# Routing of a 32-expert layer rebuilt: the second norm applied as one factor per token, logits accumulated between the projection's tiles, token rows added onto a shift row in DRAM by DMA, and slot lists found by rounding

## The reference, cut to what matters

```
x  = x + gt1 * (concat([attn, conv]) @ w_out)          # the projection w0..w7
h2 = rmsnorm(x, g_norm2) * (1.0 + sc2) + sh2           # second norm, gain, shift

logits = h2 @ w_router + b_router                      # 512 x 32
top_logit, top_idx = lax.top_k(logits, 4)
gate = softmax(top_logit)
# each expert's tokens are padded up to whole blocks of 128 slots
counts = zeros(32).at[flat_e].add(1)
padded = (counts + 127) // 128 * 128
pad_end = cumsum(padded)
slot = pad_start[e_sorted] + arange(n_pair) - start[e_sorted]
slot_tok, slot_gate = ...                              # for each slot its token and gate
block_expert = searchsorted(pad_end, block_start, side='right')

for each block:  xb = h2[tok];  y = swiglu(xb @ w_gate_up[e] + b) @ w_down[e] + b;  out[tok] += y * gate
x = x + gt2 * out;  final rmsnorm
```

## Time and profile before

| | |
|---|---|
| median of 3 runs | 2510.17 us (2509.6 to 2510.8) |
| profiled execution | 2509.06 us, its span 2507.2 us |
| PE busy in the span | 2416.3 us (96%) |
| DVE, ACT, POOL busy | 2024.9 (81%), 1320.3 (53%), 678.6 us (27%) |
| granted TensorE clock, mean | 0.98 of full speed |

### The profile page before, as it was taken

How to read it: one execution, slowest core, us unless ns; L and a number is a source line. 1 busy time by engine, 2 the same in 40 slices (tenths; PEclk the granted TensorE clock), 3 DMA queues, 4 the chain that set the end, 5 groups by cost and what they waited for, 6 DMA issues and landing times.

```text
span 2507.2 us, 31686 instructions
## 1 busy us (share of the span) xinstructions
PE 2416.3 (96%) x10915; PEld 1944.6 (78%) x10915; DVE 2024.9 (81%) x1856; ACT 1320.3 (53%) x1206; POOL 678.6 (27%) x407
## 2 busy tenths in 40 slices
PE   8999999999999999999869999999999999999995
PEld 7777788786877877878657888888888888888884
DVE  7787577576885786885269999999999999999994
ACT  4442233334323234334247777777777777777772
POOL 5343341332433432341312122112111211221120
PEclk9999999999999999999879999999999999999997
DMA  6232245222422752230069999999999999999992
GB/s 237 84 125 77 67 152 185 67 76 72 147 68 76 267 208 72 69 100 1 13 240 363 378 365 371 368 377 364 367 367 377 366 366 373 371 368 366 377 358 88
DMA packets 104427, 572.48 MB, mean 228 GB/s; under 512 B 14192, under 2 KB 14336, under 8 KB 54288
## 3 DMA queue, kind: packets, MB, share of 16 engines
q1 hardware_dynamic: 86784, 515.15, 54.9%
q0 software_dynamic: 17280, 56.20, 7.9%
q10 hardware_dynamic: 288, 0.14, 0.0%
HBM read 559.37 MB, written 24.12 MB: 233 GB/s over the span
## 4 chain that ended last, share of the span: by engine, by line
PE 86%; DVE 7%; DVEq 2%; DMA 1%; ACT 1%; issue 1%; ACTq 0%; POOL 0%; SPq 0%; POOLq 0%
PE ps L1493 83%; PE ps L1171 2%; DVE scr L2354 1%; DVE scr L2194 1%; DMA scr<-in_ada 1%; DVEq L2356 1%; DVE y_split L2131 1%; PE ps L666 0%; DVE mix L2245 0%; DVE scr L2243 0%; DMA mix<-acc_rows 0%; PE ps L1423 0%; DVEq L2141 0%; DMA acc_rows<-rows,lst 0%; DVE w_split L1298 0%
## 5 line engine op out<-in xcount | busy, mean ns | idle before, releaser
L1298 DVE TENSOR_TENSOR w_split<-raw,w_split 128x2048 fp32r<-128x2048 f32 x386 | 877.3, 2287 | 54.3 <-ACT w_split L1250 43.3
L1493 PE MATMUL ps<-y_split,pieces_split 128*128 128x512 f32 x3600 | 844.6, 395 | 15.9 <-POOLq L2561 7.3
L1250 ACT ACTIVATE w_split<-raw 128x2048 fp32r<-128x2048 f32 x386 | 736.2, 1916 | 196.0 <-PE ps L1493 176.3
L1493 PEld LDWEIGHTS ps<-y_split,pieces_split 128*128 128x128 f32 x3600 | 679.9, 189 | 167.8 <-issue 26.1
L1493 PE MATMUL ps<-w_split,rows_T 128*128 128x512 f32 x3096 | 751.9, 393 | 1.9 <-DVE rows_T L1304 1.9
L1493 PEld LDWEIGHTS ps<-w_split,rows_T 128*128 128x128 f32 x3096 | 575.3, 188 | 119.4 <-DVE rows_T L1304 2.5
L2549 POOL TENSOR_TENSOR pieces_split<-pieces,pieces_split 128x1024 fp32r<-128x1024 f32 x151 | 372.3, 2476 | 646.4 <-ACT pieces_split L1827 518.5
L1827 ACT ACTIVATE pieces_split<-pieces 128x1024 fp32r<-128x1024 f32 x144 | 151.3, 1058 | 425.6 <-PE ps L1493 394.4
L1493 PE MATMUL ps<-w_split,hidden_T 128*128 128x512 f32 x1536 | 363.6, 392 | 2.0 <-DVE hidden_T L1304 1.7
L1493 PEld LDWEIGHTS ps<-w_split,hidden_T 128*128 128x128 f32 x1536 | 284.9, 188 | 74.6 <-DVE hidden_T L1304 15.0
L1362 POOL COPY rows_i<-slot_tokens 128x1 int32 (+1 forms) x34 | 60.9, 1790 | 412.9 <-PE ps L1171 379.4
(11 more groups left out here) (265 smaller groups left out, 2068.8 us busy)
## 6 DMA issues: line engine op xcount, KB each, us to landing
raw<-in_w_moe SPq DMA_DIRECT2D x386, 1024.0 KB, 7.6
pieces<-in_pieces SPq DMA_DIRECT2D x181, 512.0 KB, 3.6
scr<-in_ada POOLq DMA_DIRECT2D x48, 512.0 KB, 5.6
scr<-in_ple SPq DMA_DIRECT2D x2, 1536.0 KB, 6.9
acc_rows<-in_zeros POOLq DMA_DIRECT2D x5, 512.0 KB, 10.9
hT<-in_xT SPq DMA_DIRECT2D x8, 256.0 KB, 5.6
h_rows<-scr SPq DMA_DIRECT2D x4, 512.0 KB, 3.7
mix<-acc_rows SPq DMA_DIRECT2D x4, 512.0 KB, 5.1
```

Of the source, the lines that this page charges most:

```text
L1250: nc.scalar.activation(wsp[:, p % SPLIT, 0], raw[:, p % RAW, :], ACT.Copy).then_inc(high, 3 if p == 1 else 1)
L1298: nc.vector.tensor_tensor(wsp[:, p % SPLIT, 1], raw[:, p % RAW, :], wsp[:, p % SPLIT, 0].bitcast(F32), ALU.subtract).then_inc(low, 3 if p ...
L1493: return pe.matmul(out, lhsT, rhs, start=start, stop=stop)
```

## The change

The shift `sh2` and the norm's factor are taken out of the path. Per token t, with 1/std the norm's factor `r`, h2 = r * (hT * coef) + sh2. So:

- ACT squares each `hT` tile and scales it by `coef` (`gained`) while PE is in the next projection tile; DVE adds up squares 1 to 6 (`sq3`). PE puts the logits' matmuls of tile k between projection tiles (from w4 on). The sums of squares come by token: 128 tokens on partitions, one column. `r_col` is 128x4 instead of 128x512. Logits are r * (gained @ w) + (sh2 @ w + bias), the latter (`shifted_bias`) made during w5 and w6.
- Token rows: ACT copies the transposed `gained` with scale `r_col`. SP has earlier written `sh2` into a DRAM row (`shift_dram`, 1024 elements of 4 bytes) and copied it to all 513 rows of `h2_dram`; POOL now adds the rows onto it by four accumulating DMAs. Rows in DRAM are numbered from 1, so that 0 means an empty slot; the count of ones is dropped from `owner`.
- Slots: `pos` in 5 wider matmuls; block counts by rounding ((n + 63.5)/128, then adding and subtracting 1.5 * 2^23); the 50 block experts by one comparison against the partition's number, one sum, and one matmul of ones against a diagonal ("be").
- Lists: block and remainder of all 16 token/choice columns at once by rounding; `in_block` in one instruction of 800 columns, then two instructions per token tile (`owner` 400 columns, `place` 512), each in buffers of its own. List matmuls have 100 columns.
- The bias load (L1120) and its splitting move from after w7 to after w0 and w4; POOL's copies ahead of the first two gathers are gone.

```diff
 def tail_sp(sp):
     for t in range(A_RAW, len(TAIL)):
+        if t == A_RAW + 2:
+            sp.wait_ge(csum_ready, 1)
+            sp.dma_start(shift_dram[0, :].rearrange("(k p) -> p k", p=P), ada[:, SH2:SH2 + DK, 0], ...)
+        if t == A_RAW + 6:
+            sp.wait_ge(h2_init, 16)
+            sp.dma_start(h2_dram[:, :], shift_dram[0, :].partition_broadcast(ROWS))
...
-    for t in range(ST):
-        sp.wait_ge(h2n_ready, t + 1)
-        sp.dma_start(h2_dram[t * P:(t + 1) * P, :], h2n[:, t, :])

 # PE
 for m_ in range(DK):
     features(CV, f"w{m_}", ...)
+    if m_ == 4:
+        router[0] = direct_router()
+        mm(ps[:, 4, 0:ST * E_N], ident[:], zer..., True, False)
+        for k in range(4):
+            pe.wait_ge(norm2_ready, GAINED(k)); logits_of(k)
+    if m_ > 4:
+        pe.wait_ge(norm2_ready, GAINED(m_ - 1)); logits_of(m_ - 1)
+    if m_ == 6:
+        pe.wait_ge(route_ready, SHIFT)
+        mm(ps[:, 5, E_N:2 * E_N], ones[:], shift_sum, True, True)
+mm(ps[:, 5, 0:ST], ident[:], zer[:, 0:ST], True, False)
+token_sums(0, False)
+pe.wait_ge(norm2_ready, SQUARED(DK - 1)); token_sums(DK - 1, True)
+pe.wait_ge(route_ready, LAST_GAINED);     logits_of(DK - 1)

 # DVE, after the logits and the top four
-            nc.vector.tensor_tensor(reached, edges, slot..., ALU.is_le)
-            nc.vector.reduce_sum(first_past, reached, AX.X)
...
+nc.vector.tensor_scalar(base, slotf, -(P - 1) / 2, 1.0 / P, ALU.add, ALU.mult)
+nc.vector.tensor_scalar(base, base, WHOLE, -WHOLE, ALU.add, ALU.add)
+nc.vector.scalar_tensor_tensor(rem, base, -float(P), slotf, ALU.mult, ALU.add)
+nc.vector.tensor_tensor(in_block[:], iota, base..., ALU.is_equal)
+for t in range(ST):
+    nc.vector.tensor_tensor(owner[:, n0:n1], in_block..., value..., ALU.mult)
+    nc.vector.tensor_tensor(place[:, n0:n1, :], iota, rem..., ALU.is_equal)
+    dve.drain().then_inc(onehot_ready, 1)

 def experts_pool(pool):
+    pool.wait_ge(h2_init, 32)
+    for t in range(ST):
+        pool.wait_ge(h2n_ready, t + 1)
+        pool.dma_start(h2_dram[1 + t * P:1 + (t + 1) * P, :], h2n[:, t, :], accum_op=ALU.add)
...
-    fetch(0, 0)
-    fetch(1, 1)
+    rows_of(list_tok[:, 0:1], 0)
+    rows_of(list_tok[:, 1:2], 1)
```

More of the change, by code:

```diff
@@ L411, in build @@
         BA = Groups(nc, ctx, "ba", [4, 5, 6, 7], ba_order)
-        CV = Groups(nc, ctx, "cv", [0, 1, 2, 3, 4, 5], [f"w{i}" for i in range(DK)] + ["logits", "pos", "lists"])
-        CA = Groups(nc, ctx, "ca", [6, 7], ["norm2"] + [f"t{i}" for i in range(8)])
+        CV = Groups(nc, ctx, "cv", [0, 1, 2], [f"w{i}" for i in range(DK)] + ["pos", "be", "lists"])
+        CA = Groups(nc, ctx, "ca", [3, 6, 7], [f"t{i}" for i in range(8)])
         DV = Groups(nc, ctx, "dv", [0, 1, 2, 3, 4, 5], [f"t{i}" for i in range(8)])
@@ L975, in tail_dve @@
             dve.sem_inc(CA.free, len(CA.banks))
+            nc.vector.memset(chosen[:, 0, :], 0.0)
+            nc.vector.memset(chosen[:, ST + 1, :], 0.0)
+            nc.vector.memset(zer, 0.0)
+            dve.drain()
             for m in range(DK):
@@ L984, in tail_dve @@
+            dve.wait_ge(std2_ready, 9)
+            nc.vector.reciprocal(r_col, std_col)
+            dve.drain().then_inc(route_ready, 1)
+            dve.wait_ge(route_full, LOGITS)
+            for t in range(ST):
+                nc.vector.scalar_tensor_tensor(logits[:, t, :], ps[:, 4, t * E_N:(t + 1) * E_N], r_col[:, t:t + 1],
+                                               shifted_bias, ALU.mult, ALU.add)
             dve.drain()
-            x = full(CV, "logits")[:, 0:ST * E_N].rearrange("p (t e) -> p t e", t=ST)
@@ L988, in tail_dve @@
-            nc.vector.tensor_tensor(logits, x, brt[:].unsqueeze(1).to_broadcast([P, ST, E_N]), ALU.add)
-            dve.drain().then_inc(CV.free, 1)
             for t in range(ST):
@@ L1035, in tail_dve @@
[L1035 to L1041 removed]
+            nc.vector.tensor_scalar(be_diag, ident[:, 0:LISTS], be_col, None, ALU.mult).then_inc(route_ready, 1)
@@ L1047, in tail_dve @@
             nc.vector.tensor_tensor(h2k, hk, posn.unsqueeze(2).to_broadcast([P, ST, TOP, E_N]), ALU.mult)
-            dve.drain()
+            nc.vector.tensor_scalar(be_bc[:], full(CV, "be", LISTS), float(E_N - 1), None, ALU.min)
+            dve.drain().then_inc(CV.free, 1)
+            nc.vector.tensor_copy(be_r[:], be_bc[0:1, :]).then_inc(be_ready, 1)
+            dve.sem_inc(low, 2)
             nc.vector.reduce_sum(slotf, hot2, AX.X)
@@ L1069, in tail_dve @@
[L1069 to L1076 removed]
+                n0, n1 = t * TOP, (t + 1) * TOP
@@ L1077, in tail_dve @@
+                nc.vector.tensor_tensor(owner[:, n0:n1], in_block[:, n0:n1, :].unsqueeze(2).to_broadcast([P, TOP, 2, LISTS]),
+                                        value[:, n0:n1, :].unsqueeze(3).to_broadcast([P, TOP, 2, LISTS]), ALU.mult)
+                nc.vector.tensor_tensor(place[:, n0:n1, :], cst[:, 0:P].unsqueeze(1).to_broadcast([P, TOP, P]),
+                                        rem[:, n0:n1].unsqueeze(2).to_broadcast([P, TOP, P]), ALU.is_equal)
                 dve.drain().then_inc(onehot_ready, 1)
-            x = full(CV, "lists")[:, 0:3 * LISTS].rearrange("p (c b) -> p c b", c=3)
@@ L1116, in bias_sp @@
         def bias_sp(sp):
-            sp.wait_ge(CV.full, CV.done(0, "w7"))
+            sp.wait_ge(CV.full, CV.done(0, "w0"))
             for i in range(2):
@@ L1354, in experts_pool @@
         def experts_pool(pool):
+            pool.wait_ge(h2_init, 32)
+            for t in range(ST):
+                pool.wait_ge(h2n_ready, t + 1)
+                pool.dma_start(h2_dram[1 + t * P:1 + (t + 1) * P, :], h2n[:, t, :], accum_op=ALU.add).then_inc(h2_out, 16)
             n = block_pairs(pool)
```

288 lines of the change are left out of this document (164 added, 124 removed).

## The result

The changed kernel takes 2477.81 us (median of 4 runs, 2476.74 to 2478.55) against 2510.01 us for the kernel before on the same chip (4 runs, 2509.6 to 2510.8): a ratio of 0.9871, 95% interval 0.9854 to 0.9888. Its profiled execution took 2478.25 us with a span of 2476.4 us, 30.81 us less than the one of before. The prediction was 2477. Medians and ranges in this document are of fast executions; one of the four of warm_hold took 6280.96 us, has no trace, and is in neither.

What follows compares the result with a forecast made beforehand. One serial chain between projection and the PE-bound expert phase was taken to bound the gain: 40.5 us for 73.45, a gain of 33; 2509.06 - 33 = 2476.1, median 1.1 above, so 2477, range 2472 to 2486.

Steps and rivals of the forecast that it cites:

- half clock: Rival: small matmuls of stages 1, 2 and 4 leave gaps, clock falls; with slow gather 2482 to 2487, chance 0.14.
- stage 4: From the lists to POOL's gather issue: 7.9 us (7.0 to 9.5), 13.21 before.
- projection, added: Router matmuls put between projection tiles, on the path: 6.5 us added; bounds 6.0, or 12.9 at half-clock price.
- stage 1: From the last projection tile to the logits: 3.5 us (3.2 to 5 if the clock falls), 31.74 before.
- stage 2: From the logits to "pos": 5.9 us (5.4 to 7), 9.44 before.
- stage 3: From "pos" to the lists: 6.1 us (5.7 to 7), 9.32 before.
- stage 5: From POOL's gather to the first expert matmul: 10.6 us (8.7 to 14.9), 9.74 before; landing taken as 6.0.
- The first weight load: SP's expert weight loads start 1.9 us after the block experts are ready, at about 1243.5.
- Late rows: Rival: the accumulating row DMAs, not the lists, set the gather: 2484, or up to 2503; chance 0.13.
- the other side: Rival: accumulating DMAs take over 13.3 us each without overlap, a loss; 2517 at 15 each; chance 0.02.
- no change: Outcome given a chance of 0.01; a measurement tells 0.2%, 5 us, from it.
- After the first expert matmul: From the first expert matmul to the end: order as before, the same 1211 us.

Runs made afterwards that it cites:

- warm_hold: Changed kernel with weight loads 3 and 4 released only after the first rows' selection, plus six unread matmuls ahead of the lists: 2476.27 us (median of three), ratio 0.9866.
- router_behind: Changed kernel with the first seven tiles' router matmuls moved from the projection to behind w7: 2480.14 us, ratio 0.9881.
- control2: The changed kernel run once more, unedited, beside all_warm: 2477.97 us, ratio 0.9867.
- control: The changed kernel run once more, unedited, on one chip with rows_first, warm_hold and bias_in_routing: 2476.14 us, ratio 0.9868.
- warm_both: Changed kernel with unread 128x512 matmuls on PE, six ahead of the lists and eight ahead of the gathered rows: 2476.48 us, ratio 0.9865.
- all_warm: warm_hold's edits on the changed kernel, plus five unread matmuls ahead of the gathered rows and two after the first bias matmul: 2471.55 us, ratio 0.9842.
- plain_rows: Changed kernel with the four row DMAs writing plainly instead of adding onto the shift, so gathered rows lack it: 2474.42 us, ratio 0.9856.
- bias_in_routing: Changed kernel with POOL's bias subtraction waiting until all eight hT tiles are done, so it runs beside the routing: 2483.23 us, ratio 0.9896.
- rows_first: Changed kernel with SP's weight loads 3 and 4 released only after the first rows' selection, so two loads stand ahead of the gather: 2475.72 us, ratio 0.9868.
- old_lists: Changed kernel with lists made as before, seven instructions per token tile and list matmuls of 150 columns instead of 100: 2479.29 us, ratio 0.9878.

## Why the prediction was right

The time of 2477 and the chance of 0.96 for faster were borne out, and of the rivals only a part of one came (half clock, in stage 4). The steps, with what each was priced at:

| step | predicted | measured |
|---|---|---|
| projection, added | 6.5 | 6.34 |
| stage 1, to the logits | 3.5 | 4.05 |
| stage 2, to "pos" | 5.9 | 6.19 |
| stage 3, to the lists | 6.1 | 6.17 |
| stage 4, lists to POOL | 7.9 | 9.67 |
| stage 5, POOL to the first matmul | 10.6 | 10.59 |
| sum | 40.5 | 43.0 |

The chain gained 30.4 us instead of 33, 2.6 short. Two things outside it nearly cancel in the profiled pair: w0's tile stands 2.00 us later than before, and from the first expert matmul to the end it takes 1209.0 us where before took 1211.4 (the prediction said "the same 1211"); together they bring the difference to 30.8. The medians differ by 32.2, 1.4 more, because the profiled execution of before lay 1.0 below its median and that of the changed kernel 0.4 above. That the median came within 1 us of 2477 is therefore in part luck.

**Projection.** The mechanism and the price of a record are right, the count was wrong. The prediction (and the text ahead of it) put 28 router matmuls ahead of w7's end; it is 24, since tile 6's stand behind w7's features. Their 48 records cost 5.30 us, 0.110 each in place of 0.108 (router_behind). The other two matmuls, with what they wait for, make up the remaining 1.04 us of the 6.34, where 0.43 was priced. The two errors nearly cancel. That nothing else there costs anything held by a hair: DVE's addition stood still for 4.66 us beside POOL's bias subtraction, and PE waited 0.22 us for it. And it did not hold in every execution: in control2 the clock fell in the projection, which the bound of 12.9 "at the half-clock price" allowed for only in the router's own records.

**Stage 1.** The four matmuls of tile 6 belong here. PE has 34 records in this window, busy 4.05 of 4.05 us, so PE sets it, not DVE's and ACT's short steps. In control and control2 the stage took 4.39 and 3.72, at 0.82 and 1.00 of full clock.

**Stages 2 and 3.** As priced, by the same steps.

**Stage 4 is the term that was mis-sized.** The prediction took 1.7 us for PE's part behind DVE, between 0.9 at full clock and 1.8 a tile at half clock. PE was granted 0.63 there, its 32 matmuls took 6.61 us from 1248.49 on, and DVE's last `place` was done at 1252.20, 2.9 us before their end. A second term in the same stage was short: from PE's end to POOL's gather it is 1.7 us, not 1.0. DVE's last instruction ends at 1255.79 and the gather's row starts 1.0 later. Before, 0.9 us lay between the end of POOL's copy (1286.27) and the gather (1287.20), so with the copy only its 0.18 us went, and not the 1.0 that stage 5 took off for it. Together that is the 1.8 by which the stage was too low (5.1 + 2.9 + 1.7 for 5.2 + 1.7 + 1.0). What the gather's wait of 0.9 to 1.0 us consists of is not shown. warm_both and all_warm show the cause of the 2.9: at full clock PE takes 1.14 us a group and waits for DVE, and the gather's issue comes 1.7 us sooner after `be_r`. So the rival of the half-clock PE came true in this one stage (9.67, its upper end was 9.5; 9.18 and 8.94 in control and control2); in stages 1 and 2 it came only in part (0.89 and 0.79 of full clock). The rival put the fall down to gaps. The trace of before shows half clock without one, in the router's matmuls:

```profile
1245.00:1250.00 5.00, 5.00 (x25) 5.00 (x25) 0.00 (x0) 0.00 (x0) 4.87 (x2) 0.50 0.00 0
```

**Stage 5.** The landing of 6.15 us was priced 6.0, but "two of the loads may still run" was not the reason. All four loads that SP may issue are ahead of the gather, and it lands when they are about through. Its reader starts 14.5 us after the first of them in this kernel, and 14.6, 14.9, 14.0, 15.4, 14.9 and 15.1 in plain_rows, router_behind, warm_both, control, control2 and bias_in_routing, though the gather was issued anywhere from 6.3 to 9.5 us after it. With two ahead (rows_first) the rows are there in 4.4, near the 4.18 of the earlier trace rows. The 6.0 held because loads and gather were both late, by 5.1 and 4.4 us, so the gap between them stayed near the one assumed (8.2 us for 8.9). The Trainium skill, page "DMA: Bandwidth & Descriptors", section "Queues, rings and completion order", says that an SDMA engine takes turns between queues packet by packet; worked out on 4.18 that gave an estimate of at most 8.4. The traces stay under it: no first gather of this study took over 7.7 us to its reader. That is no test of turns being taken, since a gather that simply ends after the four loads gives the same times. The 10.4 in the expert phase is above the bound.

**The first weight load** came 4.24 us after `be_r`, not 1.9, at 1248.58 instead of 1243.5, and this is the one new cost of the rows' addition. It is 3.55 and 3.40 us in control and control2. plain_rows puts it at about 1 to 2 us of the chain, from single traces. That SP's register loads wait behind the accumulating DMAs is what the rows suggest (2.42 us when those are plain and shorter); no run took SP's loads apart from them, so the mechanism is argued only.

**Late rows, the other side, no change.** None came: the four transfers were over by about 1250.5 (an estimate from the last issue and the median landing), some 6 us before the gather was issued.

**After the first expert matmul** 2.4 us are saved in this pair of traces, 0.9 in the control (1210.5). Over all eleven traces of changed kernels this stretch takes 1208.2 to 1210.5 us, so most of the 2.4 may be scatter of a single trace of before. In the first 96 us PE idles 3.77 us after and 4.13 before, and later 0.25 less; the rest is spread too thin to be placed. Whether it is a gain at all stays open.

## What to carry to other kernels

A serial chain between two full phases is worth every microsecond that it loses, so price it step by step, and for each step ask which engine would set it if the one named now got faster: here the lists went from DVE to PE as soon as DVE's part was cut. Here the small matmuls after waits ran at half clock; 13 unread matmuls in PE's idle time, together with letting the gather go ahead of two weight loads, were worth 5 to 6 us, though neither showed in a median alone. When a transfer at the end of a chain lands by the queue ahead of it, earlier work on the chain gains less than it saves (old_lists) until that queue is made shorter (rows_first). And take a control's trace more than once: one of three traces of the same kernel held a loss of 2.8 us that the others lack.

## What the runs showed of the hardware

**Some of DVE's instructions stand still beside POOL.** Three instructions of DVE on operands in SBUF lasted until POOL's instruction beside them was over: an addition of 128x512 took 4.66 us (0.69 otherwise) beside a subtraction of 6.80, a copy of 128x16 took 1.83 (0.17 otherwise) beside a MEMSET of 3.52, and in bias_in_routing a TENSOR_SCALAR took 6.94 (0.48 otherwise) beside a subtraction of 6.65. Others did not: beside the same MEMSET a product of 128x256 and its sum took 0.42 and 0.60 us (1223.53 and 1224.03 in the changed kernel), and in router_behind that sum took 0.62 beside the subtraction while the copy behind it took 5.89. The Trainium skill, page "SBUF — State Buffer", section "Who interferes with whom", says that DVE's second pair of ports is GpSimd's too, and that whichever instruction issues first gets it and the other blocks for the whole of it; the first two cases agree with it, as POOL's instruction stood first; in the third the two start 0.01 us apart, so it shows the block but not who was first. In the kernel before, the same POOL work ran at 1242.85 to 1253.17, while DVE waited for PE (busy 0.00 us from 1240 to 1250).

**An accumulating DMA costs more than its bytes.** Four of 512 KB moved at 206 GB/s with the DMA engines full (a DMA share of 1.07, stage 3's window), landed in 7.4 us (median; 7.4 to 9.0 in the other traces) where plain ones take 4.3, and cost POOL 0.93 to 0.84 us to issue instead of 0.56 to 0.53.

**What the clock did.** After the lists PE has 8.64 us without work in the control, and its next window (1262 to 1272) is granted 0.67; with fillers in the gaps it is 1.00. In warm_both a gap of 2.14 us after 1.06 us of transposes was followed by four microseconds at 0.50. It also fell with no gap: in control2 PE was busy for all of 1208.15 to 1212.23 with the 32 router records, granted 0.85, and the next 5.57 us, 128x512 matmuls, ran at 0.50 before the clock came back; in router_behind the 56 router records were granted 0.90 and what followed 0.50. In the other nine traces with such a run of 32 records the clock stayed at 1.00.
